# The last 256 output columns finished on GpSimd instead of VectorE, in a two-block transformer kernel

## The reference, cut to what matters

```python
h = rms_norm_2(x, g_pre_ffn[i])
x = x + rms_norm_2(swiglu(h, w_gate[i], w_up[i], w_down[i]), g_post_ffn[i])
return x
```

## Time and profile before

| what | value |
|---|---|
| median of 3 runs | 764.17 us (763.53 to 764.65) |
| time of the profiled execution | 765.39 us |
| span of the profiled execution | 763.5 us |
| TensorE matmul busy | 728.5 us, 95% of the span |
| VectorE busy | 417.9 us, 55%, 740 instructions |
| ScalarE busy | 338.3 us, 44%, 605 instructions |
| GpSimd busy | 32.8 us, 4%, 66 instructions |
| mean granted TensorE clock | 0.993 of full speed |

### The profile page before, as it was taken

One profiled execution on the slowest core, in us unless ns is written; L12 is line 12 of the kernel. 1 busy time (PEld: TensorE's weight loads), 2 busy tenths in 40 slices (PEclk: granted clock), 3 DMA queues, 4 the chain that ended last, 5 costly groups with the idle time before them and its releaser, 6 DMA issues.

```text
span 763.5 us, 12333 instructions
## 1 busy us (share of the span) xinstructions
PE 728.5 (95%) x5082; PEld 596.0 (78%) x5082; DVE 417.9 (55%) x740; ACT 338.3 (44%) x605; POOL 32.8 (4%) x66
## 2 busy tenths in 40 slices
PE   9999999999999999999787789999999999999997
PEld 8998987888888866666455459998778888888885
DVE  5677656677666511111010118676568867676766
ACT  5966665554443521111010137555667453444343
POOL 1700000000000000000000001000001000000001
PEclk9999999999999999999999999999999999999999
DMA  8963667438989999999999997954234555545101
GB/s 333 418 232 120 227 212 283 174 128 319 364 320 346 377 412 420 422 426 424 427 424 424 419 415 313 419 176 161 111 111 166 192 194 178 209 170 209 62 1 55
DMA packets 30281, 206.05 MB, mean 270 GB/s; under 512 B 3600, under 2 KB 3984, under 8 KB 11408
## 3 DMA queue, kind: packets, MB, share of 16 engines
q1 hardware_dynamic: 30224, 205.25, 68.7%
HBM read 204.18 MB, written 1.05 MB: 269 GB/s over the span
## 4 chain that ended last, share of the span: by engine, by line
PE 87%; DMA 6%; ACT 2%; DVE 2%; issue 1%; POOL 0%; SPq 0%; DVEq 0%; POOLq 0%; ACTq 0%
PE ps L782 44%; PE ps L848 10%; DMA ext<-in_dense 6%; PE ps L1210 6%; PE ps L851 5%; PE ps L1231 3%; PE ps L1132 3%; PE ps L1241 2%; PE ps L888 1%; PE ps L1046 1%; PE ps L1356 1%; ACT big L1804 1%; PE ps L1370 1%; PE ps L1331 1%; PE ps L1261 1%
## 5 line engine op out<-in xcount | busy, mean ns | idle before, releaser
L1969 DVE TENSOR_TENSOR whl<-raw,whl 128x1024 fp32r<-128x1024 f32 (+4 forms) x182 | 213.0, 1189 | 127.6 <-ACT whl L1543 126.0
L1543 ACT CAST whl<-raw 128x1024 fp32r<-128x1024 f32 (+4 forms) x182 | 181.9, 1020 | 68.7 <-PE ps L782 46.7
L782 PE MATMUL ps<-whl,fra 128*128 128x512 f32 (+2 forms) x858 | 198.7, 387 | 0.0
L782 PEld LDWEIGHTS ps<-whl,fra 128*128 128x128 f32 x858 | 156.7, 188 | 30.4 <-issue 1.0
L848 PE MATMUL ps<-fra,whl 128*128 128x512 f32 x336 | 105.5, 395 | 0.0
L782 PE MATMUL ps<-whl,frb 128*128 128x512 f32 x360 | 84.9, 390 | 0.0
L782 PEld LDWEIGHTS ps<-whl,frb 128*128 128x128 f32 x360 | 66.6, 188 | 13.2
L851 PEld LDWEIGHTS ps<-fra,whl 128*128 128x128 f32 x336 | 63.1, 188 | 14.8
L782 PE MATMUL ps<-fra,whl 128*128 128x256 f32 x552 | 69.5, 285 | 0.0
L782 PEld LDWEIGHTS ps<-fra,whl 128*128 128x128 f32 x552 | 67.1, 191 | 0.8 <-issue 0.7
L851 PE MATMUL ps<-fra,whl 128*128 128x256 f32 x336 | 66.0, 278 | 0.0
(11 more groups left out here) (300 smaller groups left out, 856.9 us busy)
## 6 DMA issues: line engine op xcount, KB each, us to landing
raw<-in_dense SPq DMA_DIRECT2D x79, 1024.0 KB, 5.2
ext<-in_dense SPq DMA_DIRECT2D x11, 2048.0 KB, 24.2
raw<-in_dense SPq DMA_DIRECT2D x5, 2048.0 KB, 31.1
ext<-in_w_down_e SPq DMA_DIRECT2D x8, 1024.0 KB, 9.5
big<-in_w_gate_e SPq DMA_DIRECT2D x7, 1024.0 KB, 27.3
big<-in_dense SPq DMA_DIRECT2D x3, 2048.0 KB, 29.1
raw<-in_dense SPq DMA_DIRECT2D x2, 3072.0 KB, 33.2
raw<-in_w_gate_e SPq DMA_DIRECT2D x5, 1024.0 KB, 7.6
```

The costliest lines, as they stand in the source:

```text
L782: t = e.matmul(o, a, w, start=first and n == 0, stop=final and n == 2, skip_group_check=not check)
L1543: e.copy(halves(q)[0], piece_view(q)).then_inc(*up("wh", q))
L1969: e.tensor_tensor(l, piece_view(q), h.bitcast(F), ALU.subtract).then_inc(*up("wl", q))
```

## The change

The last addition on VectorE, added(1, 1) for "out", covers only its first 256 columns (512 to 767). The other 256 columns (768 to 1023) of the second half of the rows are done by GpSimd at the end of its program, in two instructions: it multiplies that part of `H` by the factor of the row, in place, and then adds it to `X`. Before them it waits for gained(1, 1) and for the factor of that half, and between them for the first of the two. SP's last store waits for both engines.

```diff
             for c in range(2):
                 cols = slice(512 * c, 512 * c + 512)
                 e.wait_ge(*at("added", "out", i, c))
+                if (i, c) == (1, 1):
+                    e.wait_ge(*at("last added"))
                 load("out", ov[:, i, cols], X[:, i, cols])
...
-            def added(i, c):
-                xs = X[:, i, 512 * c:512 * c + 512]
+            def added(i, c, n=512):
+                xs = X[:, i, 512 * c:512 * c + n]
                 e.wait_ge(*at("gained " + name, i, c))
                 e.wait_ge(*at("factor", name, i))
-                e.scalar_tensor_tensor(xs, H[:, i, 512 * c:512 * c + 512], rms(name)[1][:, i:i + 1], xs, ALU.mult,
+                e.scalar_tensor_tensor(xs, H[:, i, 512 * c:512 * c + n], rms(name)[1][:, i:i + 1], xs, ALU.mult,
                                        ALU.add).then_inc(*up("added", name, i, c))
...
-            added(1, 1)
+            added(1, 1, 256 if name == "out" else 512)
...
         for i in range(2):
             root_of_means("out", i, ss[:, 2 + i:3 + i])
+        last = X[:, 1, 768:1024]
+        e.wait_ge(*at("gained out", 1, 1))
+        e.wait_ge(*at("factor", "out", 1))
+        e.tensor_scalar(H[:, 1, 768:1024], H[:, 1, 768:1024], rms("out")[1][:, 1:2], None, ALU.mult).then_inc(
+            *up("pool step", "last scaled"))
+        e.wait_ge(*own())
+        e.tensor_tensor(last, last, H[:, 1, 768:1024], ALU.add).then_inc(*up("last added"))
```

## The result

The changed kernel took 766.28 us, the median of 11 runs (764.6 to 766.71), against 764.09 of the kernel before (11 runs, 763.23 to 765.23). The ratio estimated from the runs is 1.0018, with a 95% interval of 1.001 to 1.0026, that is 0.8 to 2.0 us; it is not the plain quotient of the two medians, which would be 1.0029. So it is a little slower: the interval lies wholly above 1. The median is inside the predicted range (763.6 to 766.3), but only by 0.02 us, and above the 764.6 to 765.6 that the prediction gave to its own case.

A forecast was written before the change was run, and what follows sets the result against it. The last piece of X was taken to bound the end: with blocking, VectorE first and the scaling in between, the last store is issued at 762.02 instead of 761.06, so 764.17 + 0.96 = 765.1 us, range 763.6 to 766.3.

The forecast's parts named there:

- its own case: In the tail, GpSimd and VectorE block each other, scaling near 0.87 us: 765.1 us, range 764.6 to 765.6, chance 0.58.
- What bounds the tail: Kernel's end is set by when the last piece of X is ready; store issued 0.03 us behind, landing 2.0 later.
- The size: Last store issued at about 762.02 in place of 761.06: +0.96 us, 0.13%, forecast as no measurable change, a little slow.
- the sign of being wrong altogether: Last store issued before 761.06, or time moving by more than that issue, meaning something ahead of 759.5 has shifted.
- the rival of the dear factor: GpSimd's scaling by a factor per partition costs 4.8 ns a column, 1.46 us: 766.0 us, 0.24% slower; chance 0.18.
- GpSimd's addition: In the tail, 128x256 addition undisturbed takes 0.72 us, from 0.196 at 2 columns and 0.32 at 64, 2.05 ns a column.
- GpSimd's scaling: In the tail, 128x256 scaling undisturbed takes 0.87 us: one-immediate form at 2.2 ns a column, 0.79, plus 0.08.
- The rivals' prices: GpSimd's scaling at 256 columns: 0.39 us if cheap or all hidden (chance 0.09), 1.46 if the factor is dear (0.18).
- VectorE first after the near tie: GpSimd's scaling (759.60) and added(1, 0) (759.62) begin within 0.02 us; VectorE's reads were taken to start sooner.
- The third order: VectorE first, scaling in between: added(1, 0) to 760.37, scaling to 761.09, added(1, 1) to 761.42, GpSimd's addition to 761.99: +0.96 us.
- The rival without blocking: In the tail, both engines read side by side, GpSimd done at 761.28: +0.25 us, 764.4 us; chance 0.15.
- The cap on the other side: Fourth store moves behind the third in one DMA block, so an earlier issue is not paid out in full.

The follow-up runs named there:

- the first experiment: Changed kernel, but VectorE's two last additions read the raw sums in PSUM instead of H, so have one SBUF input; ratio 1.0005 (0.9995 to 1.0015).
- the repeat: The changed kernel as it is, timed once more against the kernel before: 765.31 us against 764.71, ratio 1.0015 (1.0005 to 1.0025).
- the four widths: Changed kernel with 64, 128, 256 (the change) or 512 columns on GpSimd; ratios against the kernel before 1.0002, 1.0000, 1.0018, 1.0027.
- the eighth experiment: Changed kernel, but ScalarE scales, GpSimd only adds, and VectorE leaves the second half's products in PSUM; ratio 0.9998 (0.9987 to 1.0010).
- the sixth experiment: Changed kernel, but VectorE adds all 512 columns again and GpSimd's scaling and addition go to scratch, the last store not waiting for them; ratio 1.0002.
- the seventh experiment: Changed kernel, but ScalarE scales the last 256 columns of H and GpSimd only adds them; ratio 1.0011 (1.0000 to 1.0022).
- the ninth experiment: Changed kernel with ScalarE scaling, products in PSUM, and the second half finished and stored in four 256-column pieces, three on VectorE, one on GpSimd; ratio 1.0013.

## Why the prediction was right, point by point

- *What bounds the tail.* Right. The last store follows the last piece of X, 0.03 behind VectorE before and 0.08 behind GpSimd after, and lands 2.0 later.
- *The size.* +0.96 at the last store was forecast, +1.00 it is in the tail, and the forecast "no measurable change, a little on the slow side" held at 1.0018, barely. The median moved by 2.19, more than the tail. That is what the prediction had named as the sign of being wrong altogether, a time that moves by more than the last issue does, and 766.28 alone would fit the rival of the dear factor (766.0) better than the forecast. Against it stand the scaling's 0.95 in the first experiment, the ratio's interval (0.8 to 2.0 us, which holds 1.00) and the repeat, whose median moved by 0.60. With 11 runs each and a head that scatters by 2 us, the three can't be told apart; a shift of some tenths ahead of the tail is not ruled out. That the median fell inside the range was luck in part.
- *GpSimd's addition.* 0.72 from the line through 2 and 64 columns, 0.72 on the chip here and in the first experiment.
- *GpSimd's scaling.* Forecast 0.87, measured 0.95 undisturbed. The slope was mis-sized: 2.5 ns a column over the four widths, where 2.2 was read from the narrow tiles, while the price of the factor was 0.05 and not 0.08. The rivals' prices, 0.39 and 1.46, are both out.
- *VectorE first after the near tie.* Right, in every width, but it was no tie: GpSimd began 0.07 behind VectorE, not 0.02 ahead, because its wait for VectorE's semaphore cost 0.17 and not 0.09.
- *The step that failed, without harm: how long each holds the other.* The third order had added(1, 1) wait for the end of the scaling, to 761.42, and GpSimd's addition wait for that in turn. In fact added(1, 1) ran to 761.05 while the scaling still ran to 761.25. It was held for 0.22 only, and so the addition started at once, at 761.34, and took its full 0.72. A row had already spoken against a hold to the end: the L1969 at 20.62 lost 0.07, though the scaling beside it ran on for 0.35 behind its start. One wait less and a longer scaling came to the same end: 762.06, on a clock that ran 0.08 later, for the forecast 761.99. The agreement to a few hundredths is partly luck.
- *The rival without blocking.* It would have been +0.25; with VectorE's second SBUF input taken away it is +0.45, so the sum of the two GpSimd instructions alone was short by 0.2 (0.08 in the scaling, 0.07 in its late start, the rest in the release of SP: the issue came 0.09 behind GpSimd's end at 761.25, where 0.03 was taken over from VectorE).
- *The cap on the other side.* Right: the eighth experiment brought the last issue 0.10 forward and won nothing at the landing.

So the loss of 1.00 divides into 0.45 for GpSimd's own path (0.95 + 0.72 and its waits, against two VectorE additions of 0.75) and 0.55 for the exclusion. Per column moved, VectorE is spared 1.05 ns (0.75 against 0.48 for 256), while GpSimd needs 2.5 + 2.1 ns. VectorE gets back little even of its 1.05: beside the scaling of 64, 128 and 256 columns added(1, 1) took 0.74, 0.73 and 0.70, where the line through 0.48 at 256 columns and 0.75 at 512 gives 0.68, 0.62 and 0.48. So it was held 0.06, 0.11 and 0.22, some 0.86 ns a column. This did not cost the tail anything by itself, since added(1, 1) was done 1.0 us before GpSimd.

## What to carry to other kernels

An idle engine is worth something only if its own path is shorter than what it takes off the other: compare the two chains from the point where both may start, not the busy shares. Before work moves to GpSimd beside VectorE, look at where VectorE's operands lie. With two in SBUF, each column that GpSimd read here was charged to VectorE too, and GpSimd waited for VectorE's whole instruction; with one in PSUM, neither happened. And where the last transfers already moved one behind the other, an earlier last issue won nothing.

## What the runs showed of the hardware that was not expected

GpSimd's scaling holds VectorE for less than its own instruction. One of 128x256 that takes 0.95 us with nothing in its way holds a two-input VectorE addition for 0.22; a GpSimd addition that reads two such tiles in 0.75 holds it for 0.46 (0.94 in place of 0.48), some twice as long. The Trainium skill (SBUF — State Buffer, section "SBUF: two separate sides") says that the one that starts first has the port for its whole instruction. For GpSimd behind VectorE the rows agree: it came through only at VectorE's end, in every width. For VectorE behind GpSimd's scaling they do not, and the measurement decides: in the sixth experiment added(1, 1) was through 512 columns at 759.27, 0.07 behind the scaling's end at 759.20, and in the changed kernel it ended 0.20 ahead of the scaling. The time fits GpSimd's reading alone, 0.86 to 0.90 ns a column and tile. That the reading is what is held is argued from these sizes and not shown directly. The one case behind a GpSimd addition does not decide: in the seventh experiment added(1, 1) ended at 760.20, 0.29 behind the addition's end at 759.91, which a hold to the end would give as well (0.33 by the prediction's reckoning).

Smaller stores did not come cheaper on SP's queue: of the four of 128x256 in the ninth experiment the first took 0.33 us, as one of 128x512 does, and the others 0.42 to 0.45. Whether their shape or their crowding is the reason was not tried.
